# A one-core hybrid recurrence block: narrow float32 products for the decay and gate columns, and a new order of the work around them in the input projection

## The reference, cut to what matters

```
qkv = silu(short_conv(qkv, conv_w))          # 3 taps along the tokens
q = l2norm(q) * HEAD_DIM ** -0.5             # over the 64 channels of a head
k = l2norm(k)
log_g = -exp(a_log) * softplus(ab[:, :, 0:2] + dt_bias)
beta  = sigmoid(ab[:, :, 2:4])
gam   = cumsum(log_g)                        # inside chunks of 64 tokens
```

## Time and profile before

| | us |
|---|---|
| median of three runs | 3588.34 |
| profiled execution, own time | 3596.93 |
| its span | 3595.1 |
| TensorE busy in the span | 3224.2 (90%) |
| VectorE busy | 2014.4 (56%) |
| ScalarE busy | 1530.2 (43%) |
| five groups for the `ab` columns, first product to first product of tile 0 | 111.81 to 137.93 |
| tiles m = 0 to 11, start | 137.93, 172.29, 203.64, 234.58, 266.71, 300.40, 329.87, 361.16, 393.26, 420.50, 445.16, 469.82 |

### The profile page before, as it was taken

How to read it: one execution, slowest core, us unless ns; L and a number is a source line. 1 busy time by engine, 2 the same in 40 slices (tenths; PEclk the granted TensorE clock), 3 DMA queues, 4 the chain that set the end, 5 groups by cost and what they waited for, 6 DMA issues and landing times. The chain is left out here.

```text
span 3595.1 us, 114044 instructions
## 1 busy us (share of the span) xinstructions
PE 3224.2 (90%) x48685; PEld 2716.6 (76%) x48685; DVE 2014.4 (56%) x3221; ACT 1530.2 (43%) x2345; POOL 1707.2 (47%) x1366
## 2 busy tenths in 40 slices
PE   6799999999997999976666659999999999999998
PEld 3677788888876999966665548778878878787877
DVE  5488620111006777767776676655565565757575
ACT  5566522333213444434444326654454452323243
POOL 0302333332005666627765185456646656556564
PEclk8899999999999999998889779999999999999999
DMA  5133443344233444445332666765565575646453
GB/s 209 51 62 81 90 97 94 108 134 136 73 101 101 143 143 143 143 127 137 107 108 71 245 219 214 248 197 195 202 220 195 196 267 189 235 163 235 181 213 122
DMA packets 458243, 556.57 MB, mean 155 GB/s; under 512 B 120980, under 2 KB 384504, under 8 KB 433528
## 3 DMA queue, kind: packets, MB, share of 16 engines
q1 hardware_dynamic: 431408, 513.19, 44.7%
q10 hardware_dynamic: 20968, 23.28, 1.9%
q0 software_dynamic: 5632, 16.78, 1.6%
HBM read 355.21 MB, written 197.97 MB: 154 GB/s over the span
## 5 line engine op out<-in xcount | busy, mean ns | idle before, releaser
L3203 PE MATMUL o_pg<-o_t_hi,o_s_hi 128*128 128x512 f32 x2016 | 793.1, 393 | 50.9 <-ACT o_part L3250 15.7
L3205 PE MATMUL o_pg<-o_t_lo,o_s_hi 128*128 128x512 f32 x2016 | 789.8, 392 | 0.0
L3206 PE MATMUL o_pg<-o_t_hi,o_s_lo 128*128 128x512 f32 x2016 | 789.3, 392 | 0.0
L601 PE MATMUL p_pg<-h_hi,p_whi 128*128 128x512 f32 (+1 forms) x1384 | 531.4, 384 | 9.6 <-DVE p_wlo L828 9.6
L601 PE MATMUL p_pg<-h_lo,p_whi 128*128 128x512 f32 (+1 forms) x1384 | 519.0, 375 | 0.0
L601 PE MATMUL p_pg<-h_hi,p_wlo 128*128 128x512 f32 (+1 forms) x1384 | 518.9, 375 | 0.0
L3203 PEld LDWEIGHTS o_pg<-o_t_hi,o_s_hi 128*128 128x128 f32 x2016 | 381.4, 189 | 142.7 <-DVE o_s_lo L3410 36.8
L3206 PEld LDWEIGHTS o_pg<-o_t_hi,o_s_lo 128*128 128x128 f32 x2016 | 381.6, 189 | 80.3
L3205 PEld LDWEIGHTS o_pg<-o_t_lo,o_s_hi 128*128 128x128 f32 x2016 | 381.4, 189 | 78.1
L3410 DVE TENSOR_TENSOR o_s_lo<-o_raw,o_s_hi 128x512 fp32r<-128x512 f32 x288 | 271.1, 943 | 198.7 <-ACT o_s_hi L3239 198.6
L601 PEld LDWEIGHTS p_pg<-h_hi,p_whi 128*128 128x128 f32 x1384 | 262.1, 189 | 61.1 <-DVE p_wlo L828 9.8
(11 more groups left out here) (353 smaller groups left out, 6442.3 us busy)
## 6 DMA issues: line engine op xcount, KB each, us to landing
o_raw<-in_w_mlp SPq DMA_DIRECT2D x32, 1024.0 KB, 5.9
scr_f<-o_xf SPq DMA_DIRECT2D x64, 512.0 KB, 7.5
o_raw<-scr_f SPq DMA_DIRECT2D x32, 1024.0 KB, 5.3
scr_w<-o_pre SPq DMA_DIRECT2D x16, 1792.0 KB, 6.5
o_t_raw<-scr_w SPq DMA_DIRECT2D x28, 1024.0 KB, 5.6
o_xf<-scr_x SPq DMA_DIRECT2D x22, 1024.0 KB, 7.8
p_raw<-in_w_in SPq DMA_DIRECT2D x38, 512.0 KB, 5.8
g_kqa<-scr_kqv SPq DMA_DIRECT2D x72, 256.0 KB, 3.0
```

Source lines behind the costliest of these rows:

```text
L601: last = nc.tensor.matmul(pg[0:m, bank, 0:n], w[:, q, k, 0:m], h[bank][:, k, :], start=(k == 0 and j == 0), stop=(k == KT - 1 and j == 2))
L3203: nc.tensor.matmul(out, s_hi[:, q, k, :], t_hi[:, q, k, :], start=(not more and k == 0), stop=False, skip_group_check=more)
L3205: nc.tensor.matmul(out, s_hi[:, q, k, :], t_lo[:, q, k, :], start=False, stop=False, skip_group_check=more)
L3206: last = nc.tensor.matmul(out, s_lo[:, q, k, :], t_hi[:, q, k, :], start=False, stop=(k == 3), skip_group_check=more)
```

## The change

In `phase_project` alone:

- **Narrow products.** The 32 columns are no longer split. TensorE multiplies the raw 32 columns in full float32 by `h_hi` and `h_lo`, with four output quarters in turn. A first step does the four 64-token pieces of the context (64 matmuls of 64 columns), a second one blocks 1 to 4, each into its own bank and quarter (64 matmuls of 512 columns). TensorE waits for the weights' transfer, no longer for the splits.
- **Next load.** SP fetches the second weight tile into `raw[:, 0]` when all narrow products are done, no longer when the split is.
- **Row chain.** The ScalarE and VectorE chain on the rows and the two scans go behind the first convolutions of tile 0.
- **Order in the tiles.** The sums, roots and norms of blocks 3 and 4 of the tile before, and the sums of block 0, move one block later. The lists are then

```diff
             def _(sp):
-                sp.wait_ge(w_lo, 1)
+                sp.wait_ge(group_full, 5)
                 sp.dma_start(raw[:, 0], win[:, :, P:2 * P]).then_inc(w_in[0], 16)
...
-                pe.wait_ge(w_lo, 1)
-                for blk in blocks_of(True):
-                    group(0, blk, P)
+                def narrow():
+                    steps = [(0, lambda q: slice(CH * q, CH * q + CH), lambda q: 0), (None, lambda q: slice(0, TB), lambda q: q + 1)]
+                    for first, cols_of, bank_of in steps:
+                        for k in range(KT):
+                            for half in (e.h_hi, e.h_lo):
+                                for q in range(4):
+                                    bank, c = bank_of(q), cols_of(q)
+                                    last = nc.tensor.matmul(pg[32 * q:32 * q + AB_W, bank, c], raw[:, 0, k, 0:AB_W],
+                                                            half[bank][:, k, c].bitcast(F32),
+                                                            start=(k == 0 and half is e.h_hi), stop=(k == KT - 1 and half is e.h_lo))
+                                    if first is None and k == KT - 1 and half is e.h_lo:
+                                        last.then_inc(group_full, 1)
+                        if first is not None:
+                            last.then_inc(group_full, 1)
+                pe.wait_ge(w_in[0], 16)
+                narrow()
...
                         group((m + 1) % 2, blk, P)
-                        if j == 0 and 1 <= m <= QK:
+                        if j == 1 and 1 <= m <= QK:
                             sums(m - 1, 3)
-                        if j == 1 and 1 <= m <= QK:
+                        if j == 2 and 1 <= m <= QK:
                             sums(m - 1, 4)
-                        if j == 1 and m < QK:
+                        if j == 2 and m < QK:
                             sums(m, 0)
...
                 for m in range(QKV):
+                    if m == 0:
+                        begin(0, 0)
+                        silu(0, 0)
+                        gate_logs()
                     split(m % 2, 16 * ((m + 2) // 2 + 1), group_no(m, 0) - 1)
-                    begin(m, 0)
+                    if m:
+                        begin(m, 0)
+                        silu(m, 0)
+                    begin(m, 1)
                     if 1 <= m <= QK:
                         root(m - 1, 3)
-                    silu(m, 0)
-                    begin(m, 1)
+                    begin(m, 2)
+                    silu(m, 1)
                     if 1 <= m <= QK:
                         root(m - 1, 4)
                     if m < QK:
                         root(m, 0)
-                    begin(m, 2)
-                    silu(m, 1)
                     begin(m, 3)
...
                 for m in range(QKV):
+                    if m == 0:
+                        conv(0, 0)
+                        gate_rows()
                     split(m % 2, m + 3)
-                    conv(m, 0)
+                    if m:
+                        conv(m, 0)
                     if 1 <= m <= QK:
                         norm(m - 1, 3)
+                    conv(m, 1)
+                    if m == 0:
+                        gate_scans()
+                    if 1 <= m <= QK:
                         norm(m - 1, 4)
                         dve.wait_ge(mul_done, 5 * m)
                         dve.sem_inc(y_ready[(m - 1) % 2], 1)
                     if m < QK:
                         norm(m, 0)
-                    conv(m, 1)
                     conv(m, 2)
```

More of the change, by code:

```diff
@@ L694, in split @@
                     nc.scalar.activation(whi[:, q, :, 0:m], raw[:, q, :, 0:m], ACT.Copy).then_inc(w_hi, 1)
-                act.wait_ge(w_in[0], 16)
-                nc.scalar.activation(whi[:, 0].rearrange("p k (q r) -> p k q r", q=4),
-                                     raw[:, 0, :, 0:AB_W].unsqueeze(2).to_broadcast([P, KT, 4, AB_W]), ACT.Copy).then_inc(w_hi, 1)
+                act.sem_inc(w_hi, 1)
                 split(1, 16, None)
@@ L711, in _, with gate_logs @@
                 act.sem_inc(ab_a, 5)
[L712 to L717, removed]
+                def gate_logs():
+                    z = ab_m
+                    nc.scalar.activation(z, ab_g, ACT.Abs).then_inc(ab_a, 1)
+                    act.wait_ge(ab_a, 6)
+                    nc.scalar.activation(z, z, ACT.Exp, scale=-1.0).then_inc(ab_a, 1)
+                    act.wait_ge(ab_a, 7)
+                    nc.scalar.activation(z, z, ACT.Ln, bias=e.ones[:, 0:1]).then_inc(ab_a, 1)
                 def begin(m, j):
@@ L825, in split @@
                                       ALU.subtract).then_inc(w_lo, 1)
[L827 to L830, removed]
+                dve.sem_inc(w_lo, 1)
                 split(1, 2)
-                g, m = ab_g, ab_m
@@ L833, in _ @@
[L833 to L851, removed]
+                def gate_rows():
+                    g, z = ab_g, ab_m
+                    dve.wait_ge(ab_a, 6)
+                    dve.tensor_scalar(g, g, 0.0, None, ALU.max).then_inc(ab_d, 1)
+                    dve.wait_ge(ab_d, 1)
+                    dve.wait_ge(ab_a, 8)
+                    dve.tensor_tensor(g, g, z, ALU.add).then_inc(ab_d, 1)
+                    dve.wait_ge(ab_d, 2)
+                    dve.tensor_scalar(g, g, e.nexpa[:, :], None, ALU.mult).then_inc(ab_d, 1)
@@ new lines, in gate_scans @@
+                def gate_scans():
+                    g, z = ab_g, ab_m
+                    dve.wait_ge(ab_d, 3)
+                    dve.memset(z, 1.0).then_inc(ab_d, 1)
+                    dve.wait_ge(ab_d, 4)
+                    dve.memset(z[:, 0:AL:CH], 0.0).then_inc(ab_d, 1)
+                    dve.wait_ge(ab_d, 5)
+                    dve.tensor_tensor_scan(ab_c, z, g, 0.0, ALU.mult, ALU.add).then_inc(ab_d, 1)
+                    dve.wait_ge(ab_d, 6)
+                    dve.memset(z[:, 0:AL:CH], 1.0).then_inc(ab_d, 1)
+                    dve.memset(z[:, CH - 1:AL:CH], 0.0).then_inc(ab_d, 1)
+                    dve.wait_ge(ab_d, 8)
+                    dve.tensor_tensor_scan(g[:, ::-1], z[:, ::-1], g[:, ::-1], 0.0, ALU.mult, ALU.add).then_inc(ab_d, 1)
```

## The result

The changed kernel is slower: 3626.26 us as the median of four runs (3621.14 to 3634.47) against 3591.85 for before with its fourth run, a ratio of 1.0087 (95% interval 1.0074 to 1.0101). By that ratio the loss is 31 us; the medians lie 34.4 apart. The forecast was 3607.5, and 3626.26 lies 1.26 us outside the range of 3599 to 3625. On another chip the same kernel gave 1.0065 (1.0050 to 1.0079). The profiled executions, 3596.93 and 3621.14 us, lie 24.2 apart.

The account below looks back on a forecast made before the run. TensorE sets the pace before, VectorE's loop with ScalarE after. Terms -10.9, -7.3, +35.6 and +0.9 sum to +18.3, taken as +19: 3616 us profiled, less 8.6 for the median, 3607.5; range 3599 to 3625.

Parts of the forecast that it names:

- What bounds the kernel: Projection: TensorE sets the pace before; after the change VectorE's loop, 36.4 us a tile with three waits for ScalarE, does.
- Narrow products, -10.9: Ahead of tile 0: narrow products end at 127.0 instead of 137.93, saving 10.9 us.
- Four at a time: Narrow products: four 32-column array tiles run side by side, 15.5 us against 62 one behind the other.
- Tile 0, -7.3: Tile 0: TensorE's 5.97 us wait for block 0's squares and about 1.3 of slow clock go; tile takes 27.1.
- Tiles 1 to 7, +35.6: Seven tiles at VectorE's loop of 36.4 us, with 2.5 added and 0.7 taken off: 256.6 against 220.97.
- The loop beside GpSimd: The tile among 1 to 7 that runs beside GpSimd: 2.5 us added to its period.
- Tiles 8 and 9, +0.9: Tile 8 goes by TensorE again, -0.6 us; tile 9 waits once for its second bank, +1.5.
- The sum, +18.3: Whole kernel: -10.9 - 7.3 + 35.6 + 0.9 us, 18 to 20 with roundings.
- the +19 that I took: Whole kernel: the sum of +18.3 taken as +19 us, putting a profiled execution at 3616.
- TensorE's waits for squares: In a q or k period, TensorE waits near 3 and 4.6 us for the squares of blocks 1 and 2.

Follow-up runs that it names:

- Roots first: Changed kernel with two swaps in ScalarE's list: root of block 3 ahead of SiLU of block 0, root of block 4 ahead of SiLU of block 1; 3572.4 us, ratio 0.9920.
- quarters in turn: Changed kernel with all 16 narrow products of one output quarter before those of the next, in both steps; ratio 1.0187 to before.
- the first four experiments: Changed kernel with old tile order, 3584.5 us; before with new order alone, 3634.47; changed kernel with two ScalarE swaps, 3572.4; changed kernel again, 3624.48.

## Why the prediction was right in kind, and 19 us short

- *What bounds the kernel*: right. VectorE's loop with ScalarE became the bound, with three waits of 3.4 to 3.5 us a tile where the prediction put them. Roots first takes two of them away and the loss with them.
- *Narrow products, -10.9*: measured -10.1 (127.82). Four at a time held. The Trainium skill, "TensorE: Matmul & The Clock Gate", Part 3, has matmuls start and end in the order of the list; the 0.86 us rows of eight records and the overlap at the borders in quarters in turn do not agree for float32 instructions of two records, and the measurement decides. That this part costs nothing elsewhere held only with the rest of the change: alone it gives 6 us back in tile 0 (40.42 against 34.36).
- *Tile 0, -7.3*: measured -7.8. The cause given was half of it: the moved chain alone takes 7.9 off and the later sum alone 7.1.
- *Tiles 1 to 7, +35.6*: the mis-sized term, measured +40.5 (261.44 against 220.97). The loop is 36.65 and not 36.4 (7 x 0.25 = 1.8). The recorded parts add up to 36.3, and the norms with their gaps take 16.2 of the measured loop where I had 15.9. Tile 1 took 37.05, 0.4 over the loop, where I had it 0.7 under (1.1). The loop beside GpSimd took 38.80 from one `norm1` to the next (265.67 to 304.47), 2.15 over and not 2.5 (-0.4). The last 2.4 lie where tile 7 hands over: it took 39.00, and the modulation sums stand between its last sum and the first product of tile 8:

```profile
376.86:415.86 39.00, 33.98 (x140) 26.40 (x139) 27.37 (x22) 22.54 (x32) 0.00 (x0) 0.89 0.32 57
```

```profile
412.43 2.08 PE L630 MATMUL p_pn<-p_s,cst 128*128 128x512 f32 x2 [4.67 <-ACT p_s L753]
414.30 1.71 PE L636 MATMUL p_pg<-cst,p_macc 128*128 128x1 f32 x8
```

Tile 3 (39.52) has these sums too, but VectorE's loop did not wait for them (36.65 from one `norm1` to the next, 229.02 to 265.67), and the tile behind it gives the time back: tile 4 took 36.46 while VectorE's loop took 38.80. Behind tile 7 TensorE sets the pace, and nothing gives it back. The prediction has no term for this hand-over. The changed kernel's granted clock was 0.91 in this stretch against 0.99 in the earlier trace rows, with TensorE busy 222.44 us against 207.80 for the same instructions. How the 2.4 splits between the sums and the clock was not tried.
- *Tiles 8 and 9, +0.9*: measured +0.6 and 0.0.
- *The sum, +18.3*: the projection's last product starts 23.2 us later (1079.5 against 1056.3), and the profiled executions are 24.2 apart, 5.2 over the +19 that I took. The other 13.7 of the miss is the level of executions. I took 8.6 off because the profiled execution of before lay that far above its median; that of the changed kernel lies 5.1 below its own. On the chip of the first four experiments, with more runs of each, the medians are 22.9 apart, close to the projection's 23.2. The range allowed for runs 7 us above 3588, which was the lowest level of before: its medians on the chips of the experiments are 3601.62 and 3598.88. Without either of the two, the 5.2 or the 13.7, the time would lie inside the range.
- *TensorE's waits for squares*: I gave 3 and 4.6 us. In tile 2 they are 1.35 and 4.66. The granted clock was 0.97 in this tile, so work at the lower clock may fill part of the first; that was not tested.

## What to carry to other kernels

When two engines hand work to each other in fixed lists, look at what the consumer still has in its own list while the producer's chain runs. A move that gives a third engine room can take that cover away, and its price is the full length of the chain (here SiLU, Square, table load, root: 3.4 us) at each place. Put the step whose input is ready ahead of the step that has to wait. A saving ahead of a serial chain can be lost if the chain's other feeders come late: here 10.7 us shrank to 4.7.

## Not expected of the hardware

- Four 32-column tiles of the array with all 128 rows run float32 products side by side at full pace: eight 512-column records in 0.86 us, where one takes 0.43.
- Order matters for it. With the quarters one behind the other, only the four records on either side of each border ran beside others, and the part took 58.5 us instead of 18.3.
- A VectorE instruction on one float32 operand of 128 x 576 in SBUF took 2.16 and 1.19 us beside GpSimd's products; in the kernel before the same two steps took 0.52 and 0.49, though the second of these also ran partly beside one. So running beside GpSimd does not decide it alone: in the changed kernel one took 0.46 us within a GpSimd product that the trace has from 135.23 to 136.94. What else it needs is open.

```profile
136.01 0.46 DVE L852 TENSOR_SCALAR p_y<-p_y 128x576 f32<-128x576 f32 x1 [1.75 <-ACT p_y L728]
```
